# An unused margin and a reordered tile: the projection operands of a two-block transformer kernel move to multiples of 512 bytes

## What is computed

```
shift, scale, gate = split(silu(c) @ w_mod + b_mod, 3)
hx = rmsnorm(x, g_pre) * (1 + scale) + shift
q, k, v, ga, uf, gf, zc, bc, cc, gc = split(hx @ w_in)      # 1024 x 2816
a = window_attention(rope(q), rope(k), v, ctx k and v, sink)
f = fourier_mix(uf, w_fourier); s = short_conv_mix(...)
y = concat(a*silu(ga), f*silu(gf), s*silu(gc)) @ w_out      # 1024 x 1024
x = x + gate * rmsnorm(y, g_post)
```

## Time and profile before

| | |
|---|---|
| three runs | 2308.47, 2313.49, 2314.11 us |
| median | 2313.49 us |
| the profiled execution: span from the first to the last instruction | 2314.2 us |
| TensorE matmuls (PE) busy | 2227.1 us, 96% |
| TensorE weight loads (PEld) busy | 2091.2 us, 90% |
| VectorE (DVE) busy | 1145.4 us, 49% |
| ScalarE (ACT) busy | 846.8 us, 37% |
| GpSimd (POOL) busy | 176.3 us, 8% |
| read from memory | 312.50 MB |

### The profile page before, as it was taken

How to read it: one execution, slowest core, us unless ns; L and a number is a source line. 1 busy time by engine, 2 the same in 40 slices (tenths; PEclk the granted TensorE clock), 3 DMA queues, 4 the chain that set the end, 5 groups by cost and what they waited for, 6 DMA issues and landing times. The chain is left out here.

```text
span 2314.2 us, 46991 instructions
## 1 busy us (share of the span) xinstructions
PE 2227.1 (96%) x19320; PEld 2091.2 (90%) x19320; DVE 1145.4 (49%) x1930; ACT 846.8 (37%) x1384; POOL 176.3 (8%) x150
## 2 busy tenths in 40 slices
PE   6999999899999999998999999999999999999998
PEld 5986798799999999976999999999999998979998
DVE  5227375653433445456653333454343446487665
ACT  4226454632221233248432222243232234455444
POOL 0003112100000010501200000010000010001000
PEclk9999999999999999999999999999999999999999
DMA  9853544445676244520354666242233233225573
GB/s 297 234 167 86 172 133 104 128 147 154 186 216 186 86 131 117 149 80 28 102 175 141 190 207 189 84 126 85 81 114 94 86 96 101 74 82 146 168 202 112
DMA packets 515900, 315.76 MB, mean 136 GB/s; under 512 B 16035, under 2 KB 513274, under 8 KB 515622
## 3 DMA queue, kind: packets, MB, share of 16 engines
q1 hardware_dynamic: 515160, 313.45, 46.1%
q10 hardware_dynamic: 590, 0.16, 0.0%
HBM read 312.50 MB, written 1.06 MB: 135 GB/s over the span
## 5 line engine op out<-in xcount | busy, mean ns | idle before, releaser
L1118 PE MATMUL ps<-h_hi,w_hi 128*128 128x256 f32 x3376 | 728.0, 280 | 3.5 <-DVE h_lo L1726 1.7
L1118 PE MATMUL ps<-h_lo,w_hi 128*128 128x256 f32 x3376 | 720.6, 278 | 0.0
L1118 PE MATMUL ps<-h_hi,w_lo 128*128 128x256 f32 x3376 | 720.6, 278 | 0.0
L1118 PEld LDWEIGHTS ps<-h_hi,w_hi 128*128 128x128 f32 x3376 | 537.8, 189 | 22.9 <-issue 21.6
L1118 PEld LDWEIGHTS ps<-h_lo,w_hi 128*128 128x128 f32 x3376 | 539.4, 189 | 0.1
L1118 PEld LDWEIGHTS ps<-h_hi,w_lo 128*128 128x128 f32 x3376 | 537.9, 189 | 0.0
L1960 DVE TENSOR_TENSOR w_lo<-stage,w_hi 128x1024 fp32r<-128x1024 f32 x227 | 285.0, 1258 | 441.5 <-ACT w_hi L1467 440.9
L1467 ACT ACTIVATE w_hi<-stage 128x1024 fp32r<-128x1024 f32 x227 | 236.6, 1055 | 334.4 <-PE ps L1118 200.4
L1960 DVE TENSOR_TENSOR w_lo<-deep,w_hi 128x1024 fp32r<-128x1024 f32 x184 | 226.1, 1234 | 226.9 <-ACT w_hi L1467 225.2
L1467 ACT ACTIVATE w_hi<-deep 128x1024 fp32r<-128x1024 f32 x184 | 191.9, 1055 | 179.7 <-PE ps L1118 141.4
L1118 PE MATMUL ps<-g_hi,w_hi 128*128 128x256 f32 x1100 | 232.9, 280 | 0.2
(11 more groups left out here) (413 smaller groups left out, 2858.0 us busy)
## 6 DMA issues: line engine op xcount, KB each, us to landing
modw<-in_ada_w SPq DMA_DIRECT2D x72, 1024.0 KB, 6.7
stage<-in_ffn_w_in SPq DMA_DIRECT2D x88, 512.0 KB, 3.9
deep<-in_ffn_w_in SPq DMA_DIRECT2D x88, 512.0 KB, 3.9
modw<-in_w_mod SPq DMA_DIRECT2D x18, 1024.0 KB, 6.1
stage<-in_w_in SPq DMA_DIRECT2D x30, 512.0 KB, 5.3
stage<-in_ffn_w_out SPq DMA_DIRECT2D x32, 384.0 KB, 3.5
stage<-in_even_w_in SPq DMA_DIRECT2D x24, 512.0 KB, 4.0
deep<-in_ffn_w_out SPq DMA_DIRECT2D x32, 384.0 KB, 3.4
```

Of the source, the lines that this page charges most:

```text
L1118: last = mm(ps[:, j, v - a:v - a + SEQ], w_part[wp][:, u % RING, c, :], x_part[xp][:, x, v:v + SEQ], start=first and wp == xp and v == a, ...
```

## The change

The margin is a new first entry of the dictionary, as long as is wanting from the first tile's address to the next multiple of 512 bytes. The token-major tile `vtok` goes from between `mixT` and `stage` to behind `modw`. All offsets are computed from the dictionary, so every tile in it moves, and those allocated behind the stretch move by the margin. No instruction is added, removed or put in another place.

```
-        sizes = {"resid": KC * NT, "big": 24 * NT, "hT": KC * NT, "mixT": KC * NT, "vtok": TT * D + TT * ML_HEADS, "stage": STAGE * KC * P,
-                 "scr": 2 * RING * KC * P, "modw": 2 * KC * SEG,
+        first = -(-nc.sbuf_base // 32) * 32
+        sizes = {"margin": (-first % BANK) // 4, "resid": KC * NT, "big": 24 * NT, "hT": KC * NT, "mixT": KC * NT, "stage": STAGE * KC * P,
+                 "scr": 2 * RING * KC * P, "modw": 2 * KC * SEG, "vtok": TT * D + TT * ML_HEADS,
                  "wfbd": 4 * P, "svec": 2 * KC * 34}
         base_of = {}
-        end = -(-nc.sbuf_base // 32) * 32
+        end = first
```

## The result

The kernel after takes 2389.79 us (median of four runs, 2388.20 to 2394.66) against 2313.01 for the kernel before (2308.47 to 2314.11, four runs): a ratio of 1.0339, 95% interval 1.0324 to 1.0354. The change costs 76.8 us, and the forecast of 2313.5, with its range to 2336, was wrong.

What follows compares the result with a forecast made beforehand. TensorE's back-to-back matmuls, 2227.1 of 2314.2 us busy, were taken to bound the kernel through their spacing. All four steps counted 0 us, so the median 2313.5 us stood as forecast, range 2281 to 2336.

Steps and rivals of the forecast that it cites:

- Step 1: Whole kernel: no instruction, wait, semaphore or queue is added, removed or moved; 0 us.
- Step 2: Spacing of the projection matmuls on TensorE: set by restarts, not by addresses; 0 us, bounds -59 and +37 us.
- bound of +37 us: Worst case for projection spacing: L1118's 7400 quick matmuls become slow, 33 us, and the seams' quick half, some 4.
- the prediction's own split: Projection matmuls: L1118 7400 quick, 6030 slow (h's 4050, g's 1980); L1162's 768 slow; 1,700 in the seams.
- bound of -59 us: Best case for projection spacing: all 15,890 matmuls fall from a mean of 115.3 ns to 111.6.
- Rival A: L1118 and L1162: with both operands on a multiple, all run at 113.3 ns; -30 us, 2284 us; chance 0.17.
- Rival A's further form: Projection matmuls: a boundary is part of the 6.6 ns too, all run at 111.6 ns; 2255 us; chance 0.06.
- Rival B: Projection matmuls: operands at the same offset meet in memory, every restart settles into 117.8 ns; +37 us, 2350 us; chance 0.11.
- 182 / 1545 in place of 170 / 1500: Sign of Rival B: stretches such as 1680 to 1850 us show the slow spacing, as us per matmul count.
- Rival C: Projection streams: spacing independent of address, but restarts shift by a few ns and some flip; 2300 to 2325 us; chance 0.26.
- Step 3: Weight transfers and the constants' 9.8 us wait at the start: 0 us, bounds 9.8 us either way.
- Step 4: ScalarE's and VectorE's conversions beside a TensorE that never idles in long stretches: 0 us, bounds 3 us either way.

Runs made afterwards that it cites:

- distance 320: Kernel after with 80 unused floats ahead of stage, so the split weights lie 320 bytes past h: 2312.9 us, ratio 1.0003 to the kernel before.
- the two halves: Two kernels, one with only the margin added (ratio 1.0001 to the kernel before), one with only vtok moved (1.032).
- the margin alone: Kernel before plus the margin, vtok left in its old place; h and g at 0, weights at 64: 2320.0 us, ratio 1.0001.
- the order alone: Kernel before with vtok moved behind modw and no margin; h, g and weights all at 128: 2392.1 us, ratio 1.032.
- the two others: The margin alone (2320.0 us, ratio 1.0001) and distance 320 (2312.9 us, ratio 1.0003), both against the kernel before.

## Why the prediction was wrong

**Step 1** (no instruction, no wait) held: the counts are the same, and TensorE's idle time fell by 4.0 us instead of rising.

**Step 2** is the step that failed: "So I read it that the way in which the stream restarts behind a stop selects the spacing". For distance 64 it was right. Both spacings occur there with the same code, as the stretches of 113.3 before and of 117.7 at distance 320 show again, and a stream does keep its value to its next stop. The conclusion that the address has no part, 0 us, did not follow. Two spacings at one address show that the address is not the only cause; they do not show that it is none. The distance sets which spacings can occur: one of 120.1 at 0, two, 113.3 and 117.7, at 64. The restart matters only where there are two. All rows of L1118 were rows of distance 64, so none of them could price another one. L1162, always at 117.5 ns at distance -64, looked like a hint in the profile and was outweighed. The runs show that it was a weak one: at the same distance the same form also ran at 113.1.

The **bound of +37 us** was too small for a separate reason. It let the matmuls spaced 113.3 ns go to 117.8 and stopped there, since 117.8 was the longest spacing in the trace. In fact those already at 117.8 had room too. By the prediction's own split: 7400 x 6.8 = 50 us from the ones at 113.3, 6030 x 2.3 = 14 from the ones of L1118 at 117.8, 768 x 2.6 = 2 from L1162, 1,700 x 4.8 = 8 from the seams; sum 74. About a quarter of the loss, by that split, is in the part that the bound held to be unable to lose. The split itself was off: by the start times 8808 of L1118's intervals are quick and 4415 slow, where mean durations rounded to a nanosecond had given 7400 and 6030. With these counts the quick ones lose 60 us and the slow ones 10.

The **bound of -59 us** rested on a row that prices something else. The 111.6 ns of L2578 are the spacing of matmuls with 129 moving columns of plain float32, not of 256 columns of float32r parts. By start times no unbroken stream of projection matmuls in the kernel before is quicker than 113.3 ns; the 112.7 and 112.9 of the prediction are that value, counted over short stretches. No distance tried has a mean below it. Rival A's further form, at 0.06, hung on the same row.

**Rival B** had the mechanism in kind, at a chance of 0.11: operands that start at the same offset, with its sign of proof, 182 / 1545 in place of 170 / 1500. The stretch went past that, to 170 / 1415. Its price of 2350 was the same bound, so the measured 2389.8 lies 40 us beyond it. That two reads meet in the memory is its reading and is not shown; shown is that the distance modulo 256 sets the spacing and that at distance 0 half as many matmuls, with half as many stationary loads, bring back 64 of the 77 us. Whether the loads and the moving reads collide, and in what, and what picks the value at 64, stays open.

**Rival A** (both on a multiple is good) is refuted by the kernel after itself, and by the two halves: offsets 0 and 64 cost what 128 and 192 cost, and 0 and 0 what 128 and 128 cost. **Rival C** is wrong in its premise that the spacing does not depend on the address. Its reshuffled restarts exist, but their size is that of the scatter at distance 64: 2311.6 to 2327.3 us for the margin alone. At distance 0, where there is one spacing, the runs of the kernel after lie between 2388.2 and 2394.7, those of the order alone between 2388.5 and 2394.2.

**Step 3** held: the constants' wait is 9.5 us for 9.8, within the 2 us. q1's packets took 43.0% of a longer span, 1027 us of the engines' time where the earlier trace rows make 1067; 4% less transfer time brought nothing that shows in the span; SP's queue waits 1564.1 us for w_lo. **Step 4** held: 1257 and 1235 ns for 1258 and 1234, and the loads of L1119 waited 1.2 us for w_lo in the form shown above.

The Trainium skill (TensorE: Matmul & The Clock Gate, Part 2, Step-by-step: what each phase is for) says that TensorE reads the moving and the stationary operand through two independent ports and that loading the next weights takes no bandwidth from the running matmul. Here the same matmuls with the same loads took 113.3 or 120.1 ns by nothing but the distance of the two operands. If the sentence is read as saying that a load costs the stream no time wherever it lies, the trace disagrees; which resource is shared is not shown. Its rule on lines of 16 bytes (SBUF — State Buffer, Door 1), on which the prediction leaned, distinguishes none of the distances tried, all multiples of 16. For alignment by itself the measured ratio of 1.0001 agrees with it. The ratios up to 1.03 show that it does not make every placement on such lines alike. The gap formula that the prediction cites (TensorE: Matmul & The Clock Gate, Back-to-back issue gap), 109.2 ns for 256 columns, is given there for an isolated matmul, not for a stream in which each has its own load; no distance tried reached it.

## What to carry to other kernels

Where every matmul loads its own stationary operand, compute the distance between the two operands modulo 256 bytes before moving a tile, and measure it as a parameter: it was worth 3.4% here, while the absolute alignment was worth nothing (ratio 1.0001). Two values at one setting do not clear the setting; a bound taken from a trace holds only for the settings that the trace contains. And the best distance belongs to the width: halving the matmuls and loads with 512 columns turned the order of distances 0 and 64 round.

## What the runs showed of the hardware

All of this is for float32r matmuls of 128 x 128 by the given columns, each with its own stationary load, at a granted clock of 1.00; the distance is stationary less moving offset modulo 256.

With 256 columns, from the stretches above: 0: 120.1 ns; 32: 118.5; 48: 117.9; 64: 113.3 or 117.7; 80: 118.9; 96: 117.5; 128: 118.8; 160: 120.1; 192: 113.3 or 117.6; 224: 116.8. Means over the whole trace, from start to start in unbroken streams of L1118's form: 0: 119.9; 32: 118.3; 48: 118.8; 64: 114.9 in the kernel before, 114.3 and 115.2 in the two others; 80: 118.8; 96: 118.1; 128: 118.7; 160: 120.0; 192: 117.0; 224: 116.9. These order the kernels' times better than a single stretch does. With 512 columns: 0: 227.0; 32: 233.8; 64: 233.8; 128: 232.8; 192: 229.2; 224: 233.8. The mean duration of a matmul follows the spacing (276, 281 and 283 ns for 113.3, 117.8 and 120.1), so the groups by form show such a shift even where no stretch is free of gaps. At least one other kind of matmul was untouched: the 32 of L2200, plain float32, took 7.17 us before and after, though their stationary tile moved from offset 192 to 0.
